# Silu as a product with a power, tile by tile: Exp on ScalarE, the rest on GpSimd

## The chip, the cores and the metric

One core of one Trainium2 chip runs the whole program in a single launch. The metric is the device time in microseconds. The engines are TensorE (PE in the rows), with its weight loads (PEld), VectorE (DVE), ScalarE (ACT), GpSimd (POOL) and SyncE (SP); each runs its own instructions in order and they meet at semaphores.

## The reference

Two transformer blocks are computed one after the other, on 512 tokens of width 1024 in float32. The change lies in the second block, in the branch beside its differential attention: a causal convolution of width 4 along the tokens, a Silu on it, and then projections to q and k of a recurrent cell:

```python
proj = u @ w_in[l]
qa, ka, va, xm, o_pre, ga, gb = jnp.split(proj, split_idx, axis=-1)
...
xc = jax.nn.silu(causal_conv(xm, conv_w, conv_b))
xch = xc.reshape(B, S, H, Dh)
q = jnp.einsum('bshd,hde->bhse', xch, w_mq)
k = jnp.einsum('bshd,hde->bhse', xch, w_mk)
```

Silu(x) is x / (1 + exp(-x)).

## The kernel before

Activations are held transposed: a tile has 128 features on the partitions and 512 tokens in its columns, so a width of 1024 is eight tiles. Each matrix product is made of three products in a rounded float format: the weights and the activations are each split into a high part (a rounded copy, made by ScalarE: `hi` for a chunk of weights, L564, and `split_hi` for an activation tile, L573) and a low part (the rest, made by VectorE: `lo`, L1925, and `split_lo`, L1931). A chunk of weights is 1024 x 128, and TensorE spends 24 products on it (L1138 to L1140).

The second attention has 32 units (four blocks of queries by eight heads). While TensorE works on a unit's scores, softmax and values, it also computes one of 32 side projections in each unit (the list `SIDE`: the two gates ga and gb, the output gate op, and xm), which fills its time. In unit i, TensorE runs projection i into bank 6 and, in the middle of it, the transposes of the weighted scores of unit i-1 (`turn`, L1692); then the scores of unit i+1 (L1684), in some units the transposes of a finished group (L1714), and the product with the values of unit i-1 (`av`, L1701). VectorE adds the mask and finds the maxima (L2469), splits weights (L1925), scales the second softmax (L2481) and writes the weighted difference of the two (L2484), which `turn` reads. ScalarE does the exponentials (L982), splits weights (L564), in every fourth unit squares and a Sqrt for the norm of a group (L955, L958), copies the transposed scores of unit i-1 (`mixed_out`, L972; `av` waits for it) and stores the side projection from the bank into a buffer (`store_side`, L949; the next projection waits for it). GpSimd sends each stored projection to memory (L2708).

The xm projections are those of units 5, 8, ... 26 (`XM_AT`). Their buffers are two (`xm_t`), taken in turn. VectorE convolves an xm tile into `E` in the three units behind it (`conv`, L2453 and L2455; semaphore `conv`). After all eight are convolved, in unit 31, ScalarE does the eight Silus in place (L993), between `mixed_out(30)` and the store of projection 31. Then, after `mixed_out(31)`, the eight tiles are split, and TensorE starts on the products for q and k, two tiles of x for each head.

The order around the Silus, on ScalarE:

```python
for i in range(UNITS + 1):
...
    if i:
        mixed_out(i - 1)
    if i == UNITS - 1:
        for kt in range(KT):
            act.wait_ge(s("conv"), kt + 1)
            A_(E[:, kt, :], E[:, kt, :], ACT.Silu).then_inc(s("xc_ready"), 1)
    if i < UNITS:
        act.wait_ge(chunk_done, C_SIDE + i + 1)
        store_side(i, bank[6][:, :])
```

Earlier in the program GpSimd has another task: it scales and adds up the modulation's weights, 128 x 1024 at a time (L2697, a multiply and an add with scalars; L2699, an add of two tiles), while VectorE works beside it on weights and hidden tiles.

Of the kernel before, what the change touches and what calls it, by code (L numbers as in the profile page):

```python
# [24 lines left out]
ALU = mybir.AluOpType  # L25
ACT = mybir.ActivationFunctionType
AX = mybir.AxisListType

P = 128
T = 512  # L30
META = 16
D = 1024
KT = D // P
# [38 lines left out]
XM_AT = [5 + 3 * k for k in range(8)]  # L72
# [6 lines left out]
def side_index(n):  # L79
    return sum(1 for x in SIDE[:n] if x[0] == SIDE[n][0])  # L80
# [65 lines left out]
def build(nc, t, out):  # L146
    ctx = ExitStack()
    with ctx:
        def sb(name, shape, dt=F32):
            return ctx.enter_context(nc.sbuf_tensor(name, shape, dt))  # L150

        def sem(name):
            return ctx.enter_context(nc.semaphore(name))

        bank = [ctx.enter_context(nc.psum_tensor(f"bank{b}", [P, T], F32)) for b in range(8)]
# [21 lines left out]
        def tiles(k, n):  # L177
            return tl(k, n).rearrange("p (a t) -> p a t", a=n)
# [25 lines left out]
        sinks = sb("sinks_b", [P, SH])  # L204
        own_head = sb("own_head", [P, 12])
        msel8 = sb("msel8", [P, P])
        eps = sb("eps", [P, 3])
        inv_d_gain = sb("inv_d_gain", [P, 16])
        gain23, wsq = inv_d_gain[:, 0:8], inv_d_gain[:, 8:16]
        comb = sb("comb", [P, 63])  # L210
# [13 lines left out]
        def s(name):  # L224
            if name not in S:
                S[name] = sem(name)
            return S[name]
# [55 lines left out]
        n = 0  # L283
# [118 lines left out]
        A, B, E = tiles(0, 8), tiles(8, 8), tiles(32, 8)  # L402
# [10 lines left out]
        pa_st = tl(42)  # L413
        xm_t = [tabs[:, k, 0:T] for k in range(2)]
        outst = [xm_t[side_index(n) % 2] if name == "xm" else tl(40 + n % 2) for n, (name, _) in enumerate(SIDE)]
        after = sb("after", [P, P])
        after_r = sb("after_r", [P, P], F32R)
# [130 lines left out]
        def _(act):  # L548
            link = Link(act, s("act_link"))
            A_ = nc.scalar.activation  # L550

            def hi(c, static=None):

                static = c if static is None else static
                if isinstance(c, int):
                    if c >= CHUNKS:
                        return
                    if c >= SPLITS:
                        act.wait_ge(chunk_done, c - SPLITS + 1)
                else:  # L560
                    i, per, base = c
                    act.wait_ge(chunk_done, i * per + (base - SPLITS + 1))
                wait_landed(act, c, static)
                A_(whi[:, static % SPLITS, :], stage[:, static % STAGES, :], ACT.Copy).then_inc(chunk_hi, 1)  # L564
# [3 lines left out]
            def split_hi(n, kt, src, shift=0.0):  # L568

                if n > 0 and kt == 0:  # L570
                    act.wait_ge(chunk_done, split_last[n - 1] + 1)
                if isinstance(shift, float):
                    ins = A_(xhi[:, kt, :], src, ACT.Copy)  # L573
                else:
                    ins = A_(xhi[:, kt, :], src, ACT.Identity, bias=shift)
                ins.then_inc(s("x_rounded"), 1)
# [362 lines left out]
            def store_side(n, b):  # L939

                if n >= 2:
                    act.wait_ge(s(f"spilled{n % 2}"), 16 * (n // 2))
                if n in XM_AT:
                    k = XM_AT.index(n)
                    if k < 2:
                        act.wait_ge(s("rot2_done"), 7)
                    else:
                        act.wait_ge(s("conv"), k - 1)
                A_(outst[n], b, ACT.Copy).then_inc(s("side_out"), 1)  # L949

            def group_squares(g):

                act.wait_ge(s("av_group"), g + 1)
                for q in range(4):
                    ins = A_(oa[g % 2][:, q * P:(q + 1) * P], bank[5][:, q * P:(q + 1) * P], ACT.Square, accum_out=ass_[:, q:q + 1])  # L955
                ins.then_inc(s("ass_ready"), 1)
                act.wait_ge(s("avar"), g + 1)
                A_(ass_[:, 4:8], ass_[:, 4:8], ACT.Sqrt).then_inc(s("astd"), 1)  # L958

            def group_out(g):  # L960
                b, hh = divmod(g, 2)
                act.wait_ge(s("oat_done"), g + 1)
                A_(A[:, 4 * hh:4 * hh + 4, b * P:(b + 1) * P], bank[7][:, :].rearrange("p (h q) -> p h q", h=4), ACT.Copy,
                   scale=sc[:, 63:64]).then_inc(s("ya_out"), 1)

            def mixed_out(i):

                b = i // AH
                act.wait_ge(s("at_t"), i + 1)
                if i >= 2:  # L970
                    act.wait_ge(s("av_done"), i - 1)
                A_(amT[i % 2][:, 0:b + 1, :], bank[4][:, 0:(b + 1) * P].rearrange("p (b q) -> p b q", q=P), ACT.Copy).then_inc(s("amt_out"), 1)  # L972

            UNITS = NB * AH
            for i in range(UNITS + 1):
                if i < UNITS:
                    b, h = divmod(i, AH)
                    N = (b + 1) * P
                    act.wait_ge(s("at_nm"), i + 1)
                    for c in range(2):  # L980
                        p = 2 * (i % 2) + c
                        ins = A_(ex[i % 2][c][:, 0:N], ex[i % 2][c][:, 0:N], ACT.Exp, bias=anm[:, p:p + 1], accum_out=asum[:, p:p + 1])  # L982
                    ins.then_inc(s("at_exp"), 1)
                    hi(C_SIDE + i + AHEAD)
                g, ph = divmod(i - 5, 4)
                if ph == 0 and 0 <= g < 7:
                    group_squares(g)
                if i:
                    mixed_out(i - 1)
                if i == UNITS - 1:  # L990
                    for kt in range(KT):
                        act.wait_ge(s("conv"), kt + 1)
                        A_(E[:, kt, :], E[:, kt, :], ACT.Silu).then_inc(s("xc_ready"), 1)  # L993
                if i < UNITS:
                    act.wait_ge(chunk_done, C_SIDE + i + 1)
                    store_side(i, bank[6][:, :])
                if ph == 0 and 0 <= g < 7:
                    group_out(g)


            for kt in range(KT):
                act.wait_ge(s("xc_ready"), kt + 1)
                split_hi(5, kt, E[:, kt, :])
            for m in range(3):
                if m == 2:
                    act.wait_ge(s("xm_in"), 16)
                    for kt in range(KT):
                        split_hi(6, kt, Dt[:, kt, :])
                for pair in range(2):
                    c = C_QKV + 2 * m + pair  # L1010
                    hi(c + AHEAD)
                    for q in range(4):
                        if q < 3:
                            act.wait_ge(s("qkv_done"), 3 * (c - C_QKV) + q + 1)
                        else:
                            act.wait_ge(chunk_done, c + 1)
                        A_((Ct, B, Dt)[m][:, 4 * pair + q, :], bank[q][:, :], ACT.Copy).then_inc(s("qkv_out"), 1)
                    if c == C_QKV:
                        group_squares(7)
                    if c == C_QKV + 1:  # L1020
                        group_out(7)
# [889 lines left out]
        def _(dve):  # L1911
            V = nc.vector
            link = Link(dve, s("dve_link"))
# [58 lines left out]
            V.memset(eps[:, 0:1], EPS1)  # L1972
            V.memset(eps[:, 1:2], EPS2)
            V.memset(eps[:, 2:3], EPS1 * EPS2)
            V.memset(comb[:, :], 0.0)
            V.memset(ss5, 1.0)
            link(V.memset(sc[:, 0:1], 0.0))
# [318 lines left out]
            for c in range(C_OUT1, C_FF1):  # L2296
                if c > C_OUT1:
                    lo(c + AHEAD)
                n = c - C_OUT1
# [137 lines left out]
            UNITS = NB * AH  # L2437
# [211 lines left out]
        def _(pool):  # L2649
            G = nc.gpsimd  # L2650
            link = Link(pool, s("pool_link"))
# [36 lines left out]
            for n in range(total):  # L2688
                m, kt = divmod(n, KT)
# [16 lines left out]
            for n, (name, _) in enumerate(SIDE):  # L2706
                pool.wait_ge(s("side_out"), n + 1)
                pool.dma_start(spill[name][side_index(n)], outst[n]).then_inc(s(f"spilled{n % 2}"), 16)  # L2708
            for q in range(2):
                pool.wait_ge(s(f"spilled{q}"), 8 * len(SIDE))  # L2710
            pool.wait_ge(s("av_done"), NB * AH)
# [54 lines left out]
```

## Time and profile before

| what | us |
|---|---|
| time, median of 3 runs | 2012.9 |
| lowest and highest run | 2012.11, 2016.67 |
| span of the profiled execution | 2012.8 |
| TensorE busy in it | 1962.5 (97%) |
| VectorE, ScalarE, GpSimd busy | 1144.1, 786.4, 366.4 |

The profile is of one execution, whose span is the time from its first to its last instruction. A row of a timeline gives a start and a duration in us, and in brackets how long the engine stood idle before it and for whom. Matmul rows overlap, so their spacing tells more than their duration. The second attention runs from about 1144 to 1391 us of the span.

### The profile page before, as it was taken

The numbers are of one execution on the slowest core, as the hardware profiler recorded it, in microseconds if no ns is written. First come the engines' busy times: TensorE is split into PE (matmuls) and PEld (weight loads), VectorE is DVE, ScalarE is ACT, GpSimd is POOL, SyncE is SP. The second block draws the span as 40 slices with busy tenths as digits, with TensorE's granted clock in tenths as the row PEclk, the third lists the DMA queues.
The fourth block names the chain that finished last, engine by engine and source line by source line (L and its number), as shares of the span: only waits on it lengthen the run. The fifth ranks groups of instructions, "written<-read, shape, count | busy, mean of one in ns | idle before, by whom it ended". The sixth has DMA issues, their size and how long they took to land.

```text
span 2012.8 us, 25489 instructions
## 1 busy us (share of the span) xinstructions
PE 1962.5 (97%) x9512; PEld 1572.4 (78%) x9512; DVE 1144.1 (57%) x1762; ACT 786.4 (39%) x1330; POOL 366.4 (18%) x298
## 2 busy tenths in 40 slices
PE   8999999999999999999999999999999999999998
PEld 6876678888887788888788877777677788888887
DVE  7566667667666655353564266665635755444444
ACT  7436442223225222222332345557756442222223
POOL 3000039999100694000000000000001000000000
PEclk9999999999999999999999999999999999999999
DMA  6320246666322664323245433323126423333331
GB/s 167 89 70 22 62 139 204 203 201 206 122 84 75 177 204 130 104 86 102 84 136 124 120 115 109 107 94 126 55 87 195 121 77 101 88 104 88 100 98 59
DMA packets 274989, 233.12 MB, mean 116 GB/s; under 512 B 16631, under 2 KB 248442, under 8 KB 274368
## 3 DMA queue, kind: packets, MB, share of 16 engines
q1 hardware_dynamic: 255792, 166.29, 28.3%
q0 software_dynamic: 17488, 60.36, 9.5%
q10 hardware_dynamic: 1632, 5.45, 1.1%
q8 instruction: 48, 0.79, 0.2%
q14 instruction: 29, 0.24, 0.0%
HBM read 214.95 MB, written 12.58 MB: 113 GB/s over the span
## 4 chain that ended last, share of the span: by engine, by line
PE 89%; DVE 5%; ACT 3%; issue 1%; DMA 1%; ACTq 0%; DVEq 0%; POOLq 0%
PE bank L1138 25%; PE bank L1140 24%; PE bank L1139 24%; PE bank L1144 2%; PE bank L1145 2%; DVE wlo L1925 1%; PE bank L1684 1%; PE bank L1701 1%; PE bank L1586 1%; PE bank L1842 1%; PE bank L1825 1%; PE bank L1355 1%; PE bank L1194 1%; PE bank L1507 1%; PE bank L1403 1%
## 5 line engine op out<-in xcount | busy, mean ns | idle before, releaser
L1138 PE MATMUL bank<-xhi,whi 128*128 128x512 f32 x1680 | 666.5, 397 | 5.5 <-PE bank L1701 2.4
L1140 PE MATMUL bank<-xhi,wlo 128*128 128x512 f32 x1680 | 656.4, 391 | 0.0
L1139 PE MATMUL bank<-xlo,whi 128*128 128x512 f32 x1680 | 655.3, 390 | 0.0
L1925 DVE TENSOR_TENSOR wlo<-stage,whi 128x1024 fp32r<-128x1024 f32 x309 | 406.4, 1326 | 207.7 <-ACT whi L564 207.3
L564 ACT ACTIVATE whi<-stage 128x1024 fp32r<-128x1024 f32 x309 | 321.2, 1051 | 403.3 <-PE bank L1140 365.0
L1138 PEld LDWEIGHTS bank<-xhi,whi 128*128 128x128 f32 x1680 | 316.3, 188 | 76.8 <-issue 9.9
L1140 PEld LDWEIGHTS bank<-xhi,wlo 128*128 128x128 f32 x1680 | 316.0, 188 | 68.1
L1139 PEld LDWEIGHTS bank<-xlo,whi 128*128 128x128 f32 x1680 | 316.4, 188 | 63.4
L2316 DVE SCALAR_TENSOR_TENSOR H<-bank,sc,H 128x512 f32<-128x512 f32 x304 | 217.9, 747 | 78.4 <-PE bank L1140 76.6
L1138 PE MATMUL bank<-hidhi,whi 128*128 128x512 f32 x532 | 209.5, 394 | 0.0
L1140 PE MATMUL bank<-hidhi,wlo 128*128 128x512 f32 x532 | 208.4, 392 | 0.0
L1139 PE MATMUL bank<-hidlo,whi 128*128 128x512 f32 x532 | 206.8, 389 | 0.0
L2338 DVE TENSOR_TENSOR arena<-bank,arena 128x512 f32<-128x512 f32 x44 | 30.5, 692 | 310.0 <-PE bank L1140 308.3
L2699 POOL TENSOR_TENSOR arena<-arena 128x1024 f32<-128x1024 f32 x63 | 167.9, 2666 | 5.3
L2684 POOL DMA_DIRECT2D arena<-in_w_ada x72 | 42.3, 588 | 430.6 <-DVE xlo L1931 259.0
L1140 PEld LDWEIGHTS bank<-hidhi,wlo 128*128 128x128 f32 x532 | 99.9, 188 | 23.2
L1139 PEld LDWEIGHTS bank<-hidlo,whi 128*128 128x128 f32 x532 | 99.9, 188 | 22.3
L1138 PEld LDWEIGHTS bank<-hidhi,whi 128*128 128x128 f32 x532 | 100.0, 188 | 20.3
L2697 POOL TENSOR_SCALAR arena<-arena,sc 128x1024 f32<-128x1024 f32 x72 | 105.1, 1460 | 5.6 <-DMA arena<-in_w_ada 2.5
L860 ACT ACTIVATE hidhi<-arena 128x512 fp32r<-128x512 f32 x44 | 27.9, 633 | 195.7 <-DVE arena L2338 195.7
L855 ACT ACTIVATE arena<-bank 128x512 f32<-128x512 f32 x44 | 26.4, 600 | 150.9 <-PE bank L1140 150.9
L2708 POOL DMA_DIRECT2D spill_ga<-arena x8 | 4.4, 552 | 415.3 <-ACT arena L949 415.3
(447 smaller groups left out, 2072.5 us busy)
## 6 DMA issues: line engine op xcount, KB each, us to landing
arena<-in_w_ada POOLq DMA_DIRECT2D x72, 512.0 KB, 4.0
stage<-in_w_in SPq DMA_DIRECT2D x71, 512.0 KB, 3.9
stage<-in_w_ff SPq DMA_DIRECT2D x64, 512.0 KB, 4.5
stage<-in_w_gate SPq DMA_DIRECT2D x44, 512.0 KB, 4.5
stage<-in_w_up SPq DMA_DIRECT2D x44, 512.0 KB, 3.9
stage<-in_w_down SPq DMA_DIRECT2D x44, 512.0 KB, 3.8
arena<-arena ACTq DMA_DIRECT2D x16, 256.0 KB, 5.4
stage<-in_w_proj_a SPq DMA_DIRECT2D x8, 512.0 KB, 4.1
```

The lines of the kernel that those rows point to most:

```text
L564: A_(whi[:, static % SPLITS, :], stage[:, static % STAGES, :], ACT.Copy).then_inc(chunk_hi, 1)
L1138: mm(out, sh, mh, start=start, stop=False, **kw)
L1139: mm(out, sh, ml, start=False, stop=False, **kw)
L1140: return mm(out, sl, mh, start=False, stop=stop, **kw)
L1144: mm(out, sh, mh, start=start, stop=False)
L1145: mm(out, sl, mh, start=False, stop=False)
L1925: V.tensor_tensor(wlo[:, static % SPLITS, :], stage[:, static % STAGES, :], whi[:, static % SPLITS, :].bitcast(F32), ALU.subtract).then_in ...
L2316: V.scalar_tensor_tensor(out=H[:, x, :], in0=bank[(4 + x) % 8][:, :], scalar=gate(x), in1=H[:, x, :], op0=ALU.mult, op1=ALU.add).then_inc( ...
L2338: V.tensor_tensor(hid_t[j], bank[2 * j + 1][:, :], act_t[j], ALU.mult).then_inc(hid_f32, 1)
L2684: pool.dma_start(st_ada[n % 3], t["w_ada_2"][0, kt * P:(kt + 1) * P, m * D:(m + 1) * D]).then_inc(ring[n % 3], 16)
L2697: link(G.tensor_scalar(dst, st_ada[n % 3], silu_c[:, kt:kt + 1], 0.0, ALU.mult, ALU.add))
L2699: G.tensor_tensor(acc, acc, t_ada, ALU.add).then_inc(s("ada_sum"), 1)
```

## The change

The Silu is taken apart. In units 9, 12, ... 30, one unit after a tile's convolution is finished, ScalarE writes exp(-x) into the xm buffer of that tile, which its spill and its convolution have read by then. GpSimd, behind the spill of the same unit, adds 1, takes the power -1 (against a column of -1 spread over the tile) and multiplies into `E`. The store of a later xm tile into the same buffer now waits for GpSimd's product. Behind the last unit ScalarE splits two tiles before `mixed_out(31)`, two after it, then stores projection 31, then splits the other four.

```diff
-        eps = sb("eps", [P, 3])
+        eps = sb("eps", [P, 4])
...
-                        act.wait_ge(s("conv"), k - 1)
+                        act.wait_ge(s("xc_ready"), k - 1)
...
+                if i == UNITS:
+                    for kt in range(2):
+                        act.wait_ge(s("xc_ready"), kt + 1)
+                        split_hi(5, kt, E[:, kt, :])
                 if i:
                     mixed_out(i - 1)
-                if i == UNITS - 1:
-                    for kt in range(KT):
-                        act.wait_ge(s("conv"), kt + 1)
-                        A_(E[:, kt, :], E[:, kt, :], ACT.Silu).then_inc(s("xc_ready"), 1)
-                if i < UNITS:
+                if i - 4 in XM_AT:
+                    k = XM_AT.index(i - 4)
+                    act.wait_ge(s("conv"), k + 1)
+                    A_(xm_t[k % 2], E[:, k, :], ACT.Exp, scale=-1.0).then_inc(s("xc_exp"), 1)
+                if i < UNITS - 1:
                     act.wait_ge(chunk_done, C_SIDE + i + 1)
                     store_side(i, bank[6][:, :])
...
-            for kt in range(KT):
+            for kt in range(2, KT):
                 act.wait_ge(s("xc_ready"), kt + 1)
                 split_hi(5, kt, E[:, kt, :])
+                if kt == 3:
+                    store_side(UNITS - 1, bank[6][:, :])
...
+            V.memset(eps[:, 3:4], -1.0)
...
                 pool.wait_ge(s("side_out"), n + 1)
                 pool.dma_start(spill[name][side_index(n)], outst[n]).then_inc(s(f"spilled{n % 2}"), 16)
+                if n - 4 in XM_AT:
+                    k = XM_AT.index(n - 4)
+                    e = xm_t[k % 2]
+                    pool.wait_ge(s("xc_exp"), k + 1)
+                    link(G.tensor_scalar(e, e, 1.0, 1.0, ALU.add, ALU.mult))
+                    link(G.tensor_tensor(e, e, eps[:, 3:4].to_broadcast([P, T]), ALU.pow))
+                    G.tensor_tensor(E[:, k, :], E[:, k, :], e, ALU.mult).then_inc(s("xc_ready"), 1)
```

## Rows read from the trace of the kernel before

**Rows 1.** The page: the span, and TensorE's busy time, share and instructions.

```profile
span 2012.8 us, 25489 instructions
...
PE 1962.5 (97%) x9512; PEld 1572.4 (78%) x9512; DVE 1144.1 (57%) x1762; ACT 786.4 (39%) x1330; POOL 366.4 (18%) x298
```

**Rows 2.** Stretches: length, each engine's busy time, TensorE's granted clock, DMA share, GB/s.

```profile
1150.00:1380.00 230.00, 225.37 (x1089) 169.50 (x1088) 141.51 (x373) 124.93 (x296) 16.88 (x31) 0.99 0.34 106
...
1387.00:1395.00 8.00, 4.57 (x19) 3.49 (x18) 4.11 (x7) 8.00 (x16) 1.46 (x2) 0.79 0.19 58
```

**Rows 3.** Timeline, TensorE, end of the attention: start, duration, line, tiles, idle before.

```profile
1385.31 0.39 PE L1139 MATMUL bank<-xlo,whi 128*128 128x512 f32 x1
1385.54 0.39 PE L1140 MATMUL bank<-xhi,wlo 128*128 128x512 f32 x1
...
1386.65 0.60 PE L1692 MATMUL bank<-ident,arena 128*128 128x128 f32 x4
1390.39 1.24 PE L1701 MATMUL bank<-arena 128*128 128x128 f32 x8 [3.13 <-ACT arena L972]
...
1392.49 0.63 PE L1139 MATMUL bank<-xlo,whi 128*128 128x512 f32 x1
1392.91 0.63 PE L1140 MATMUL bank<-xhi,wlo 128*128 128x512 f32 x1
```

**Rows 4.** Timeline, ScalarE, units 30 and 31 and the splits behind them.

```profile
1377.84 0.60 ACT L949 ACTIVATE arena<-bank 128x512 f32<-128x512 f32 x1 [1.86 <-PE bank L1140]
...
1383.81 1.28 ACT L993 ACT_TABLE_LOAD   x1
1385.11 4.27 ACT L993 ACTIVATE arena<-arena 128x512 f32<-128x512 f32 x8
...
1389.76 0.58 ACT L972 ACTIVATE arena<-bank 128x512 f32<-128x512 f32 x1
1390.24 4.26 ACT L573 ACTIVATE xhi<-arena 128x512 fp32r<-128x512 f32 x8
```

**Rows 5.** VectorE: the subtractions behind the splits (timeline), L1925 over the span (min/median/max ns).

```profile
1390.89 4.91 DVE L1931 TENSOR_TENSOR xlo<-arena,xhi 128x512 fp32r<-128x512 f32 x8 [5.14 <-ACT xhi L573]
...
L1925 DVE TENSOR_TENSOR wlo<-stage,whi x309: 1210/1224/3415, 12.5 to 1980.6; 128x1024 fp32r<-128x1024 f32 x155
```

**Rows 6.** Timeline, ScalarE: the stores of units 9, 11 and 27.

```profile
1214.37 0.60 ACT L949 ACTIVATE arena<-bank 128x512 f32<-128x512 f32 x1 [0.62 <-PE bank L1140]
...
1228.83 0.60 ACT L949 ACTIVATE tabs<-bank 128x512 f32<-128x512 f32 x1 [2.39 <-PE bank L1140]
...
1352.61 0.60 ACT L949 ACTIVATE arena<-bank 128x512 f32<-128x512 f32 x1 [2.17 <-PE bank L1140]
```

**Rows 7.** Timeline, GpSimd and VectorE behind the store of unit 30.

```profile
1378.73 0.54 POOL L2708 DMA_DIRECT2D spill_op<-arena  x1 [7.87 <-ACT arena L949]
...
1382.95 1.23 DVE L1925 TENSOR_TENSOR wlo<-stage,whi 128x1024 fp32r<-128x1024 f32 x1 [2.54 <-ACT whi L564]
...
1385.00 0.75 DVE L2484 SCALAR_TENSOR_TENSOR arena<-arena,small 128x512 f32<-128x512 f32 x1
```

**Rows 8.** GpSimd's two operations over the whole span: count, min/median/max ns, first, last.

```profile
L2697 POOL TENSOR_SCALAR arena<-arena,sc x72: 1127/1133/3182, 282.9 to 777.2; 128x1024 f32<-128x1024 f32 x72
...
L2699 POOL TENSOR_TENSOR arena<-arena x63: 2399/2412/3281, 287.0 to 778.5; 128x1024 f32<-128x1024 f32 x63
```

**Rows 9.** Timeline, GpSimd and VectorE side by side in the first block.

```profile
388.34 1.20 POOL L2697 TENSOR_SCALAR arena<-arena,sc 128x1024 f32<-128x1024 f32 x1
...
388.73 1.88 DVE L1925 TENSOR_TENSOR wlo<-stage,whi 128x1024 fp32r<-128x1024 f32 x1 [0.18 <-ACT whi L564]
...
389.62 3.24 POOL L2699 TENSOR_TENSOR arena<-arena 128x1024 f32<-128x1024 f32 x1
```

**Rows 10.** Timeline, TensorE: the transposes that need the weighted scores of units 10 and 28.

```profile
1225.64 0.38 PE L1692 MATMUL bank<-ident,arena 128*128 128x128 f32 x2
...
1365.97 0.60 PE L1692 MATMUL bank<-ident,arena 128*128 128x128 f32 x4
```

## The prediction

> **What bounds the kernel now.** I read the page first: a span of 2012.8 us and TensorE busy for 97% of it [rows 1]. So a change pays only where TensorE stands still, and costs only where it makes TensorE stand still. I then asked for the stretch that the diff touches, engine by engine. In the second attention, from 1150 to 1380 us, TensorE is busy 225.37 of 230 us and GpSimd 16.88 us, all of it the issuing of spills; from 1387 to 1395 us TensorE is busy only 4.57 of 8 us, at a granted clock of 0.79 [rows 2]. Next, the order of TensorE's work in that hole: the last transposes of the weighted scores (L1692) start at 1386.65 us and take 0.60, then it idles 3.13 us for ScalarE's copy of them (L972), does the last product with the values (L1701, 1.24 us), idles 0.30, and does six products at a spacing of 0.43 us, where it had 0.23 before the idle time [rows 3]. ScalarE's rows say why: after the copy for unit 30 it loads a table (1.28 us), does the eight Silus (4.27 us, 0.53 each), stores the last side projection, and only at 1389.76 copies for unit 31 [rows 4]. The Silus are the cause of the hole. The rest of the attention is bound by TensorE.
>
> **What the change takes away at the end.** The table load and the eight Silus leave that place, and the last store moves behind four splits. ScalarE then does two splits of x (0.53 us each) once projection 31 is done, near 1386.0, and has finished them when the transposes end at 1387.25. Its copy (0.58 us) ends at about 1387.95 and TensorE goes on at 1388.0 where it went on at 1390.39: 2.4 us won. VectorE subtracts behind each split at 0.61 us (4.91 us for eight, [rows 5]), so the first two tiles wait for nothing. If an idle time of 0.7 us leaves the clock up, six products at 0.23 for 0.43 give another 1.2. So the gain has a floor near 2.4 and a roof of 3.6 us.
>
> **What it adds on ScalarE.** Eight Exps of one 128x512 tile, at some 0.6 us like a store of that size [rows 4], in units 9, 12, ... 30. Ahead of the store of unit 27 ScalarE idles 2.17 us and ahead of that of unit 30 1.86 [rows 6, 4]; the Exp fits in. In units 9 and 21 a Sqrt stands before it, so the table load that now comes with the next softmax is drawn ahead: 1.28 + 0.6 = 1.9 us against 0.62 us of idle time in unit 9 [rows 6]. The store then ends some 1.3 us later; TensorE has the scores, a group's transposes and the values to do before it wants that bank, so I price it at 0 to 0.3 us, and take 0. One wait changes its meaning: the store of an xm tile waits for GpSimd's product of two tiles before, not for the convolution. The last spill is issued some 0.4 us earlier, and the read of xm that follows it is wanted only after four more chunks of products, so it keeps its room.
>
> **What it adds on GpSimd.** Three instructions for each tile, behind the spill of units 9, 12, ... 30. From the end of ScalarE's store of unit 30, 1378.44 us, it takes 0.29 us to the spill's issue and 0.54 for it [rows 4, 7]. 1+e is a two-step operation on 1024 columns at 1.13 us at the least, so about 0.57 on 512; the product at the end is half of 2.40, or 1.2 us [rows 8]. With two short gaps the power starts 1.5 us behind the store. No row shows a power. From below, it can't be quicker than that two-input operation: 1.2 us. From above, no row bounds it; I build it from L2697: two steps for 1024 columns in 1.13 us are 0.28 us for one step on 512. A power is a logarithm, a product and an exponential, each with a polynomial, a splitting of exponent and digits, and the special cases: I count some 42 steps, and would believe 28 to 64. That is an estimate of 12 us, from 8 to 18. I take 12, as the row nearest in kind is the same engine's arithmetic, not ScalarE's table.
>
> Whether that hurts is decided by VectorE. Where GpSimd runs beside it, one of the two stands still: L1925, two inputs in SBUF, normally 1.22 us, was at work from 388.73 for 1.88 us while L2697 ran until 389.54, which is the wait for its end and 1.07 us more; GpSimd's next operation was then stretched from 2.41 to 3.24 us [rows 8, 9]. The longest L1925 took 3.4 us [rows 5]. So I let VectorE's two-input operations wait for the whole power. The Trainium skill, SBUF — State Buffer, section "SBUF: two separate sides", calls the shared pair an exclusive lock held for the full instruction; the rows show that for operations of up to 2.4 us, and no row shows it for a long one.
>
> Who waits: L1925 of the next unit stands at the head of VectorE's queue, and behind it the scaling of the second softmax (L2481) and the weighting (L2484), and these make what TensorE transposes. In unit 31 L1925 starts at 1382.95 and the weighting ends at 1385.75 [rows 7]. After a power ends, VectorE needs about 1.1 us for L1925, lets GpSimd's product pass (1.2, partly beside small operations), and 1.2 for L2481 and L2484: 3.4 us. Free room is then the time from the store's end to TensorE's transposes, less 1.5 + 3.4. For the tile of unit 9: 1225.64 - 1214.97 - 4.9 = 5.8 us; for that of unit 27: 1365.97 - 1353.21 - 4.9 = 7.9; for that of unit 30: 1386.65 - 1378.44 - 4.9 = 3.3 [rows 3, 4, 6, 7, 10]. The same subtraction for units 12, 15, 18, 21 and 24 gives 6.3, 6.3, 6.3, 6.7 and 8.2.
>
> **The sum.** With 12 us for a power the first seven tiles cost 6.2 + 5.7 + 5.7 + 5.7 + 5.3 + 3.8 + 4.1 = 36.5 us, the last 8.7. Each stall of the first seven also drops the clock for some six products: 7 x 1.2 = 8.4 [rows 3]. At the end 2.4 is won; the clock falls there as before. 2012.8 + 36.5 + 8.7 + 8.4 - 2.4 = 2064. The span and the median of the runs (2012.9) are 0.1 us apart, so I leave it at 2064. With 8 us: 8.7 + 4.7 + 6 (five stalls with a fall of the clock) - 2.4 gives 2030; with 18 us: 78.5 + 14.7 + 8.4 - 2.4 gives 2112. GpSimd's spills of the two units behind come late by some 16 us, but the buffer that they free is wanted three units on, 24.6 us after the store of unit 27 [rows 4, 6].
>
> **Rivals.** (a) The power is cheap, up to 3.3 us. Then no tile waits, and the end gains 2.4 to 3.6: 2009.2 to 2010.4. It decides below 3.3 us. For it speaks that GpSimd stands idle and the tiles are three units apart; against it, that a two-input add alone takes 1.2 us. (b) A middle price, 3.3 to 7 us, if steps in a long program overlap so that one costs 0.14 us rather than 0.28 (42 steps: 5.9 us). Seven tiles are nearly hidden, and the last one's stall eats the gain: 5.9 - 3.3 - 2.4 = +0.2, so 2013. The Trainium skill's GPSIMD Engine Reference, section "Elementwise — side-by-side cycle accounting", has long bodies bound at roughly three operations a cycle of 1.2 GHz; by that an estimate for 42 steps is 6.0 us, and the time 2013. (c) The power holds VectorE up only while it fetches, not throughout. Then the return of the tile decides: 1.5 + 12 + 0.1 + 1.2 = 14.8 us behind the store of its unit; the buffer is wanted by the store two units on, which starts 13.9 us behind the end of unit 9's store [rows 6] and later than that for the rest, less some 1.2 us that TensorE has in hand; and the last tile is wanted by the last split near 1391.1, with some 2 us of cover from the first chunk's products. With 12 us that gives 2010 to 2013; with 18 us (20.8 us of return) about 5 us on six tiles and 7 at the end less 2.4, some 2045. Against it stand rows 9. (d) More than 64 steps: over 2112.
>
> **How the numbers follow.** The forecast, 8 to 18 us with the hold, has a chance of 0.45 (2030 to 2112). Cheap (a) 0.17, middle (b) 0.13, no hold (c) 0.13, dearer (d) 0.12. The predicted time is the forecast's, 2064. The range leaves out (d) and the edge of (a): 2008.5 to 2112. A measurement of this kernel can tell about 0.2%, 4 us, from no change. Faster by more needs all of the gain's roof and a little over, so half of (a) and little of (b) and (c): 0.13. Within 4 us: the rest of (a), most of (b), half of (c): 0.23. Slower: 0.45 + 0.12 and the rests of (b) and (c): 0.64.
>
> **What would show it.** The tensor-power rows on GpSimd give the price at once: about 12 us, eight of them. Beside each, one L1925 of VectorE should be as long as what is left of the power, and TensorE should idle for the weighting 4 to 6 us in the mid of the unit after next, at a lower clock behind it. At the end TensorE should wait about 0.7 us for the copy L972 once the transposes are done. The prediction is wrong if the power rows are under 7 us, or if L1925 keeps to 1.2 us beside a long one; then look at the xm stores in ScalarE's queue and at the last split.

## The result and the profile after

The changed kernel takes 2574.8 us (median of four runs, 2573.55 to 2580.6) where the kernel before takes 2014.52 beside it: a ratio of 1.2787, 95% interval 1.2769 to 1.2806. The forecast was 2064 us, the range ended at 2112. The sign was right, and the size was off by a factor of eleven (560 us against 51).

The page of the changed kernel: span, busy time of each engine, and the group of GpSimd that was not there before (count, then busy us and mean ns).

```profile
span 2571.7 us, 25512 instructions
...
PE 1977.2 (77%) x9512; PEld 1585.1 (62%) x9512; DVE 1146.2 (45%) x1763; ACT 784.7 (31%) x1329; POOL 1036.4 (40%) x322
...
L2721 POOL TENSOR_TENSOR tabs<-tabs,eps 128x512 f32<-128x512 f32 x8 | 655.6, 81949 | 0.7
```

Against [rows 1], VectorE and ScalarE have the same work as before; GpSimd has 670 us more, 655.6 of them in eight powers. One power of a 128x512 tile takes 81.95 us. It was the operation that no row of the kernel before showed and that the forecast put at 12 us.

GpSimd's timeline around the first tile (start, duration, line; in brackets the idle time before and its cause) shows what a power blocks:

```profile
1213.09 0.54 POOL L2715 DMA_DIRECT2D spill_ga<-arena  x1 [8.00 <-ACT arena L949]
1213.66 0.63 POOL L2720 TENSOR_SCALAR tabs<-tabs 128x512 f32<-128x512 f32 x1
1214.38 81.96 POOL L2721 TENSOR_TENSOR tabs<-tabs,eps 128x512 f32<-128x512 f32 x1
1296.42 1.26 POOL L2722 TENSOR_TENSOR arena<-arena,tabs 128x512 f32<-128x512 f32 x1
1297.62 0.63 POOL L2715 DMA_DIRECT2D spill_gb<-arena  x1
1298.70 0.55 POOL L2715 DMA_DIRECT2D spill_xm<-tabs  x1 [0.46 <-ACT tabs L949]
```

The spill of the next unit waits from about 1220 to 1297 us behind the power, and the store of the xm tile two units on waits for the product at 1296.42: it starts at 1297.79, and TensorE goes on at 1298.44. The waits of TensorE and of ScalarE over the attention (us in total, times, longest):

```profile
PE bank L1144 <- ACT tabs L949: 415.3, 6, 71.3
PE bank L1144 <- issue: 69.8, 1, 69.8
PE bank L1144 <- ACT arena L949: 61.9, 3, 61.2
...
ACT tabs L949 <- POOL arena L2722: 432.3, 6, 74.3
ACT xhi L573 <- POOL arena L2722: 71.8, 1, 71.8
ACT arena L949 <- DMA spill_op<-arena: 64.0, 1, 64.0
```

These eight waits are the loss. Six times ScalarE's store of an xm tile waits for GpSimd's product in the same buffer, and TensorE waits for the store: 415.3 us. Once (the tile of unit 27, whose buffer no later xm tile wants) the store of unit 30 waits for the spill of unit 28, which stood in GpSimd's queue behind the power: 61.2 us. And the last tile makes the last split late by 71.8 us. In ScalarE's queue the copies out of the banks (L1023) stand behind that split, and TensorE goes on at 1954.82, after the first of them: 69.8 us. The profile names no cause for this wait; ScalarE's rows give it:

```profile
1952.66 0.63 ACT L573 ACTIVATE xhi<-arena 128x512 fp32r<-128x512 f32 x1 [71.78 <-POOL arena L2722]
...
1954.15 2.04 ACT L1023 ACTIVATE arena<-bank 128x512 f32<-128x512 f32 x4
```

Together 415.3 + 61.2 + 69.8 = 546.3 us. TensorE's busy time has grown by 1977.2 - 1962.5 = 14.7 us. Part of that is the lower clock after each wait, here after the first (stretch, length, busy time of PE, PEld, DVE, ACT and POOL, then TensorE's granted clock, DMA share, GB/s):

```profile
1298.40:1301.60 3.20, 3.16 (x8) 2.49 (x9) 1.25 (x2) 1.91 (x5) 0.55 (x1) 0.50 0.43 164
1302.00:1306.00 4.00, 4.00 (x21) 2.99 (x20) 1.93 (x4) 0.91 (x3) 0.00 (x0) 1.00 0.46 133
```

After 71.28 us of standing still TensorE runs at 0.50 of full speed, 1.2 GHz, for some 3.2 us and then at 2.4 GHz. The hole of 3.13 us [rows 3] has shrunk to 0.69, so 2.4 us less. 2012.8 + 546.3 + 14.7 - 2.4 = 2571.4, against a span of 2571.7. That the sum closes so well is partly luck: between executions without any such wait the busy time differs by up to 9 us (1957.0 us in the run silu_tile below, 1965.8 in tanh).

VectorE, which the forecast had made the sufferer, wasn't held. L1931 is the split of weights (L1925 before); first all of it between 1205 and 1960 us (min/median/max ns), then one that ran inside the first power:

```profile
L1931 DVE TENSOR_TENSOR wlo<-stage,whi x25: 1224/1226/1309, 1207.4 to 1959.7; 128x1024 fp32r<-128x1024 f32 x25
...
1215.40 1.23 DVE L1931 TENSOR_TENSOR wlo<-stage,whi 128x1024 fp32r<-128x1024 f32 x1 [2.11 <-ACT whi L564]
```

At 1215.40, 1 us into a power that lasts until 1296.34, it takes its 1.23 us. The contrast with [rows 9] is what the experiments had to explain.

### The profile page after: what moved, and what is told of

Same layout as the page of the kernel before. It is cut to its first block, busy times and chain, and to the rows that moved or that the text cites. A ratio compares the mean times of both kernels' runs of the same rounds, so it can differ in the third digit from the quotient of the medians.

```text
span 2571.7 us, 25512 instructions
## 1 busy us (share of the span) xinstructions
PE 1977.2 (77%) x9512; PEld 1585.1 (62%) x9512; DVE 1146.2 (45%) x1763; ACT 784.7 (31%) x1329; POOL 1036.4 (40%) x322
## 4 chain that ended last, share of the span: by engine, by line
PE 65%; POOL 23%; DVE 4%; issue 4%; ACT 2%; DMA 1%; ACTq 0%; DVEq 0%; POOLq 0%
POOL tabs L2721 22%; PE bank L1144 19%; PE bank L1146 18%; PE bank L1145 18%; PE bank L1150 1%; PE bank L1151 1%; DVE wlo L1931 1%; PE bank L1592 1%; PE bank L1848 1%; PE bank L1361 1%; PE bank L1831 1%; PE bank L1200 0%; PE bank L1513 0%; PE bank L1409 0%; DMA arena<-spill_pa 0%
## 5 line engine op out<-in xcount | busy, mean ns | idle before, releaser
L1144 PE MATMUL bank<-xhi,whi 128*128 128x512 f32 x1680 | 674.4, 401 | 551.6 <-ACT tabs L949 415.3
L1931 DVE TENSOR_TENSOR wlo<-stage,whi 128x1024 fp32r<-128x1024 f32 x309 | 407.1, 1328 | 681.2 <-ACT whi L564 680.9
L2721 POOL TENSOR_TENSOR tabs<-tabs,eps 128x512 f32<-128x512 f32 x8 | 655.6, 81949 | 0.7
```

The source lines that it names most:

```text
L1144: mm(out, sh, mh, start=start, stop=False, **kw)
L1931: V.tensor_tensor(wlo[:, static % SPLITS, :], stage[:, static % STAGES, :], whi[:, static % SPLITS, :].bitcast(F32), ALU.subtract).then_in ...
L2721: link(G.tensor_tensor(e, e, eps[:, 3:4].to_broadcast([P, T]), ALU.pow))
```

## The experiments

The first four runs below are one execution each, beside one of the kernel before (2016.2 us). All executions of that kernel lie between 2010.0 and 2019.7 us, so where a time differs from it by less than some 10 us, only the rows decide.

Two theories stood after the result. A: a power has a high price for each column, leaves VectorE alone, and costs what its late return makes others wait. B: the forecast's own step, that VectorE is held by it. Beside them: that the price is fixed for an instruction or belongs to this exponent, these numbers or this form of operand, and that the rest of the change costs something too.

**What a power costs (cols).** The power becomes a power to 1 on a part of each tile, and a Tanh makes the Silu right without it.

```diff
-  A_(xm_t[k % 2], E[:, k, :], ACT.Exp, scale=-1.0)
+  A_(xm_t[k % 2], E[:, k, :], ACT.Tanh, scale=0.5)
...
-  V.memset(eps[:, 3:4], -1.0)
+  V.memset(eps[:, 3:4], 1.0)
...
-  link(G.tensor_scalar(e, e, 1.0, 1.0, ALU.add, ALU.mult))
-  link(G.tensor_tensor(e, e, eps[:, 3:4].to_broadcast([P, T]), ALU.pow))
+  link(G.tensor_scalar(e, e, 1.0, 0.5, ALU.add, ALU.mult))
+  w = (512, 256, 128, 64, 32, 16, 4, 1)[k]
+  link(G.tensor_tensor(e[:, 0:w], e[:, 0:w], eps[:, 3:4].to_broadcast([P, w]), ALU.pow))
```

> Base: Tanh in place of Exp and 0.5(1+e) in place of the power, so that the tiles come out right; then a power (to 1, which changes nothing) on the first 512, 256, 128, 64, 32, 16, 4 and 1 columns of tile 0, 1, ... 7. Theory A (the price is per column, 81.95/512 = 0.16 us each, and what it costs is the tile's late return): powers of 82, 41, 20.5, 10.2, 5.1, 2.6, 0.6 and 0.2 us; TensorE idles 71 us for the return of tile 0, 29 for tile 1, 8 to 9 for tile 2, nothing from 64 columns down; time 2013 + 109 + 3 clock losses of 1.8 - 3.6, some 2123. Rival C (most of the price is fixed for an instruction): all eight near 80 us, time near 2570. Rival B (the power stops VectorE's two-input operations): beside the 512-column power one of L1925's rows is tens of us long.

The timeline of GpSimd, the eight powers alone, and TensorE's wait for the stores:

```profile
1216.08 81.97 POOL L2722 TENSOR_TENSOR tabs<-tabs,eps 128x512 f32<-128x512 f32 x1
...
1310.53 41.15 POOL L2722 TENSOR_TENSOR tabs<-tabs,eps 128x256 f32<-128x256 f32 x1
...
1364.64 20.74 POOL L2722 TENSOR_TENSOR tabs<-tabs,eps 128x128 f32<-128x128 f32 x1
...
1398.61 10.55 POOL L2722 TENSOR_TENSOR tabs<-tabs,eps 128x64 f32<-128x64 f32 x1
...
1423.46 5.45 POOL L2722 TENSOR_TENSOR tabs<-tabs,eps 128x32 f32<-128x32 f32 x1
...
1445.57 2.93 POOL L2722 TENSOR_TENSOR tabs<-tabs,eps 128x16 f32<-128x16 f32 x1
...
1471.63 1.03 POOL L2722 TENSOR_TENSOR tabs<-tabs,eps 128x4 f32<-128x4 f32 x1
...
1496.86 0.57 POOL L2722 TENSOR_TENSOR tabs<-tabs,eps 128x1 f32<-128x1 f32 x1
...
PE bank L1144 <- ACT tabs L949: 108.3, 3, 71.3
```

A straight line: 81.97 - 41.15 = 40.82 us for 256 columns, 0.159 us each, and about 0.4 us for the instruction. Of the three waits, 71.3 us belong to 512 columns; TensorE's idle times in the same trace give 29.2 us for 256 and 7.8 for 128, where theory A said 29 and 8 to 9, and from 64 columns down no store is waited for. The time is 2128.32 us against 2123 expected, 112 over the kernel before beside it against 110 expected. So a wait follows from the length of the power and the room of the tile, as rival (c) of the forecast has it; the price put into that rule was wrong.

**Does the price depend on what is raised to what (forms)?** With the Tanh, eight operations of 64 columns on a scratch tile:

```diff
+  by = [eps[:, c:c + 1].to_broadcast([P, 64]) for c in range(3, 7)]
+  b_, r_ = base[:, :], res[:, :]
...
+  if k == 0:
+      link(G.tensor_tensor(r_, b_, by[0], ALU.pow))
+  elif k == 1:
+      link(G.tensor_tensor(r_, b_, expo[:, :], ALU.pow))
+  elif k == 2:
+      link(G.tensor_tensor(r_, b_, by[1], ALU.pow))
...
```

> Same base with Tanh; beside the right result GpSimd does one 64-column operation on a scratch tile for each of the eight tiles, and nobody reads it: power by -1 from a spread column, -1 from a full tile, 2, 0.5, 1, -1 of a tile of ones, -1 on 16 partitions only, and an add. Theory A, a fixed program per column: the six on 128 partitions all 10.2 us whatever exponent, number or operand form; the one on 16 partitions the same (each core does its own partitions); the add under 0.4 us. Rival C2 (the price is that of the special exponent, of the numbers or of the spread operand): the rows differ by a factor of two or more. Time: each return is 1.5 + 0.3 + 10.2 + 0.8 + 1.3 = 14.1 us against 13.9 to 16.5 of room, so nothing is waited for: 2009 to 2013.

GpSimd's groups (lines in no order of time; L2734 is -1, L2736 -1 from a full tile, L2738 2, L2740 0.5, L2742 1, L2744 a tile of ones, L2746 16 partitions, L2748 the add):

```profile
L2736 POOL TENSOR_TENSOR res<-base,expo 128x64 f32<-128x64 f32 x1 | 10.6, 10587 | 0.1
L2744 POOL TENSOR_TENSOR res<-base,eps 128x64 f32<-128x64 f32 x1 | 10.6, 10582 | 0.1
L2734 POOL TENSOR_TENSOR res<-base,eps 128x64 f32<-128x64 f32 x1 | 10.6, 10567 | 0.1
L2740 POOL TENSOR_TENSOR res<-base,eps 128x64 f32<-128x64 f32 x1 | 10.6, 10558 | 0.1
L2746 POOL TENSOR_TENSOR res<-base,eps 16x64 f32<-16x64 f32 x1 | 10.6, 10555 | 0.1
L2738 POOL TENSOR_TENSOR res<-base,eps 128x64 f32<-128x64 f32 x1 | 10.5, 10549 | 0.1
L2742 POOL TENSOR_TENSOR res<-base,eps 128x64 f32<-128x64 f32 x1 | 10.5, 10547 | 0.1
...
L2748 POOL TENSOR_TENSOR res<-base,expo 128x64 f32<-128x64 f32 x1 | 0.3, 317 | 0.1
```

All seven powers take 10.55 to 10.59 us: none of the four exponents is a short cut, a tile of ones is no cheaper, and 16 partitions cost what 128 do. The add takes 0.32. The time is 2013.93 us beside 2016.2 of the kernel before. ScalarE's stores wait for a tile four times (10.4 us in all, 3.2 at most), but TensorE has work for so long: it waits for such a store once, 0.26 us. So seven powers of 10.6 us cost almost nothing, and are near the edge.

**Does a power hold VectorE (aside)?** The kernel before, and on GpSimd eleven powers that nobody waits for:

```diff
   pool.dma_start(spill[name][side_index(n)], outst[n]).then_inc(s(f"spilled{n % 2}"), 16)
+  if 9 <= n < 30 and n % 2:
+      link(G.tensor_tensor(aside[:, :], aside[:, :], eps[:, 3:4].to_broadcast([P, 80]), ALU.pow))
```

> The kernel before, with its Silus where they were; GpSimd does, behind the spills of units 9, 11, ... 29, a power on 80 columns of a scratch tile that nobody reads: eleven of 12.8 us, the price that the forecast took. Theory A (VectorE isn't held): time of the kernel before, within 2 us, and L1925 at 1.22 us throughout. Rival B (VectorE's two-input operations wait for the power): each power ends 13.7 us behind its store, the weighted scores come at 16 us against 10.7 to 13.1: 3 to 5 us eleven times and a fall of the clock each, some 2065, and eleven L1925 of 8 to 11 us.

The power (min/median/max ns) and the split of weights (here L1926) between 1200 and 1450 us:

```profile
L2713 POOL TENSOR_TENSOR aside<-aside,eps x11: 13125/13126/13235, 1216.2 to 1371.3; 128x80 f32<-128x80 f32 x11
...
L1926 DVE TENSOR_TENSOR wlo<-stage,whi x30: 1221/1226/1227, 1204.6 to 1428.0; 128x1024 fp32r<-128x1024 f32 x30
```

Eleven powers of 13.13 us, and the longest of the 30 splits takes 1.227. The time is 2015.16 us, beside 2016.2. Theory B falls: with powers of about the price that the forecast took (12 us), VectorE's splits lose nothing.

**And an ordinary stream (aside_mul)?** The same places, five products of 1024 columns instead:

```diff
+  if 9 <= n < 30 and n % 2:
+      aside = hidhi[:, :, :].rearrange("p a t -> p (a t)")
+      for _ in range(5):
+          link(G.tensor_tensor(aside, aside.bitcast(F32), ones[:, 0:1].to_broadcast([P, 1024]), ALU.mult))
```

> The same with five two-input products of 1024 columns (2.4 us each, 12 us together) in place of each power, on a hidden tile that is not in use then, multiplied by ones. If what held VectorE in the first block is a two-input stream of GpSimd: L1925 up to 3.4 us and others likewise in the units with products; a unit's chain of VectorE is 3 to 6 us longer against 4 to 5 us of room, so the time is 0 to 20 us over that of the kernel before. If GpSimd's work beside the attention held VectorE in general, the powers of the run beside this one do the same.

GpSimd's five products and VectorE's operations beside them (timeline), then what TensorE waited for:

```profile
1229.67 10.18 POOL L2712 TENSOR_TENSOR hidhi<-hidhi,ones 128x1024 fp32r<-128x1024 f32 x5
...
1229.42 2.19 DVE L2479 TENSOR_TENSOR small<-small,sc 128x1 f32<-128x1 f32 x1
1231.64 2.06 DVE L2481 TENSOR_SCALAR arena<-arena,small 128x256 f32<-128x256 f32 x1
1233.74 2.07 DVE L2484 SCALAR_TENSOR_TENSOR arena<-arena,small 128x256 f32<-128x256 f32 x1
...
1238.02 0.41 DVE L2469 CUSTOM_DVE_ANT_0 arena<-bank,arena 128x256 f32<-128x256 f32 x1
...
PE bank L1692 <- DVE arena L2484: 23.0, 10, 4.0
PE bank L1701 <- ACT arena L972: 14.9, 11, 3.5
PE bank L1714 <- DVE gg L2444: 10.8, 5, 3.4
```

An operation of VectorE on a single column, 0.16 us in the runs with a power, takes 2.19 beside a product of 2.03 us (the mean of all 55); each of the next two waits for one product too. Not every operation is held: L2469, which reads a bank of TensorE and a tile, keeps its 0.41 us while the last product still runs, and none of its 46 rows between 1200 and 1450 us is longer than in the kernel before (0.69 us). TensorE waits ten times for the weighted scores, as the forecast described it. The time is 2074.23 us, 58 over the kernel before, more than the 0 to 20 that I expected; the rows show small operations held for a whole product each. So the hold is real, it comes with the products and not with the powers, and for like durations (10 to 13 us in every second unit) the products cost 58 us and the powers nothing that can be told.

**What the rest of the change is worth (tanh, tanh_old_end).** Without a power, with Tanh as above; the second also goes back to the old order behind the last unit:

```diff
-                if i == UNITS:
-                    for kt in range(2):
-                        act.wait_ge(s("xc_ready"), kt + 1)
-                        split_hi(5, kt, E[:, kt, :])
...
-                if i < UNITS - 1:
+                if i < UNITS:
...
-                if kt == 3:
-                    store_side(UNITS - 1, bank[6][:, :])
```

> The change without a power: Silu(x) = x * 0.5 * (1 + tanh(x/2)), Tanh on ScalarE in the Exp's place, 0.5(1+e) and the product on GpSimd. Theory A (the power is the whole loss, and the rest is worth what the end of the attention gives): 2.4 to 3.6 us under the kernel before, ratio 0.9982 to 0.9988. Rival D (the eight functions in ScalarE's units, GpSimd's products or the new order cost too): the same as before or slower.

> The same with the old order behind the last unit: store 31, the copy for unit 31, then the eight splits. If the gain is the removal of the Silus from there, this keeps all but 0.5 us of it, as the copy starts when the transposes end and the first split comes at 1388.4 by the clock of the kernel before, with its subtraction at 1389.0, about when TensorE has the values done. If the two early splits are what wins, it loses 1 us or more of it.

The ratios are 0.9993 (0.9982 to 1.0004) and 0.9987 (0.9975 to 0.9999). So what is left of the change is a gain of some 0.1%, which in the changed kernel's own order can't be told from none, and the two orders can't be told apart by time. The trace with the old order has the same idle time of 0.69 us ahead of the last product with the values as the changed kernel. The two early splits win nothing that can be seen.

**Silu itself, moved (silu_tile, silu_old_end).** No Exp, nothing on GpSimd; the Silu of each tile in the Exp's place, with the new order and with the old one:

```diff
-  A_(xm_t[k % 2], E[:, k, :], ACT.Exp, scale=-1.0).then_inc(s("xc_exp"), 1)
+  A_(E[:, k, :], E[:, k, :], ACT.Silu).then_inc(s("xc_ready"), 1)
...
```

> Silu itself in the Exp's place, tile by tile on ScalarE, nothing on GpSimd. Each brings two table loads of 1.28 us, one ahead of it and one ahead of the next softmax. ScalarE's idle time ahead of the store is 1.9 to 2.4 us in most of these units, the softmax has 4 to 5 us of room: if these rooms are right, 2 to 3.6 us are won as with Tanh. If the softmax is late (its room was misread), 1.3 us are lost eight times: 7 us slower than with Tanh.

> Silu tile by tile on ScalarE in the middle of the attention, as in the run silu_tile, and the old order behind the last unit: nothing is left of the change but where the Silus stand. If the hole behind the Silus was the whole gain to be had (3.6 us), this has it: TensorE idles 0.7 us for the last copy and goes on at the full clock, ratio 0.998 to 0.9995. If the early splits were needed, TensorE idles 1 us or more before the products for q.

0.9987 (0.9976 to 0.9999) and 0.9982 (0.9972 to 0.9992): the second is 2011.26 us beside 2015.3. It beats both kernels, and it differs from the kernel before only in where the eight Silus stand (and in an unused column of constants). The wait for the last copy, and, from the run silu_tile, ScalarE's rows in a unit with a Silu:

```profile
PE bank L1701 <- ACT arena L972: 0.7, 1, 0.7
...
1347.23 1.28 ACT L997 ACT_TABLE_LOAD   x1
1348.53 0.64 ACT L997 ACTIVATE arena<-arena 128x512 f32<-128x512 f32 x1
1349.36 0.60 ACT L949 ACTIVATE arena<-bank 128x512 f32<-128x512 f32 x1 [0.20 <-PE bank L1146]
1349.98 1.28 ACT L982 ACT_TABLE_LOAD   x1
```

The table load and the Silu fill the time in which ScalarE would have idled before its store, and the load back falls into the room of the softmax.

**The reciprocal on VectorE (recip).** In place of GpSimd's three operations:

```diff
+  dve.wait_ge(s("xc_exp"), k + 1)
+  link(V.tensor_scalar(e, e, 1.0, None, ALU.add))
+  link(V.reciprocal(e, e))
+  V.tensor_tensor(E[:, k, :], E[:, k, :], e, ALU.mult).then_inc(s("xc_ready"), 1)
```

> Exp on ScalarE as in the change; 1+e, reciprocal and product on VectorE in the unit behind, nothing on GpSimd. No row shows a reciprocal of 512 columns; the 4-column ones take 0.18 us. At one column a cycle as the other operations, the three take 0.35 + 0.6 + 0.7 us and fit in VectorE's room of 4 to 5 us: 2.4 to 3.6 us won. If the reciprocal takes 4 us or more, up to 1 to 3 us are lost in each of eight units and it is slower than before.

The reciprocal's row (min/median/max ns):

```profile
L2504 DVE RECIPROCAL tabs<-tabs x8: 3352/3352/3354, 1219.7 to 1409.4; 128x512 f32<-128x512 f32 x8
```

3.35 us is under the 4 us from which I expected a loss, and still the ratio is 1.0113 (1.0092 to 1.0134): 23 us over the kernel before, an expectation that missed. The loss isn't even. TensorE waits 18.6 us in six places for the scaling of a finished group (L2451), where the kernel before has 2.0; in the two longest, 5.8 and 6.2 us, a reciprocal stands ahead of that scaling in VectorE's queue. So the room of 4 to 5 us that I took for every unit wasn't there in these two.

## Why the prediction was right or wrong

- **The hole behind the Silus: right in the rows, its worth borne out by another run.** TensorE's rows at the end of the changed kernel's attention:

```profile
1876.57 0.60 PE L1698 MATMUL bank<-ident,arena 128*128 128x128 f32 x4
1877.86 1.16 PE L1707 MATMUL bank<-arena 128*128 128x128 f32 x8 [0.69 <-ACT arena L972]
1879.32 0.47 PE L1144 MATMUL bank<-xhi,whi 128*128 128x512 f32 x1 [0.30 <-DVE xlo L1937]
1879.62 0.40 PE L1145 MATMUL bank<-xlo,whi 128*128 128x512 f32 x1
```

  0.69 us of idle time instead of 3.13 [rows 3], and a granted clock of 1.00, 2.4 GHz, from 1876 to 1885 us, where [rows 2] has 0.79 over the hole. That is the roof of 3.6 us, and silu_old_end measures 4 us, with an interval from 1.6 to 5.6 (0.9982 of 2015). The changed kernel's own end, in the run tanh, gives 0.7 in a thousand, which can't be told from nothing.
- **What it adds on ScalarE: right.** The Exp makes the store of unit 9 late, and TensorE waits 0.24 us for it, within the 0 to 0.3 us allowed; no later unit shows such a wait, in the run tanh neither, where no power hides one.
- **GpSimd around the power: right.** The power of the second tile starts 1.57 us behind its store (1.5), 1+e takes 0.63 us (0.57), the product 1.26 (1.2).
- **The price of the power: the step that failed.** I counted 42 steps at 0.28 us for 512 columns. 81.95 us are some 290 such steps. With the price goes the range: its upper end, 18 us, was only the upper end of the count. The count was a guess about a program whose length no row shows, and the bounds of 28 to 64 gave a guess the look of a range; an operation without a row should have been left open above, with the point where it begins to cost (some 14 us of return) as the only firm number. The Trainium skill's GPSIMD Engine Reference, section "Elementwise — side-by-side cycle accounting", has about three operations a cycle for long bodies; my 42 steps at that rate gave an estimate of 6.0 us, and the measured 82 us decide against the count, the rate or both.
- **VectorE held for the whole power: the second step that failed.** All the stalls of the sum were of this kind (36.5 us for the first seven tiles, 8.7 for the last), and none of them happened. (The terms of the 3.4 us behind a power add up to 3.5, which changes little.) The rows of before were read rightly and carried over to an operation of another kind. aside_mul has the hold, aside and the changed kernel have not: 1.23 us for a split beside powers of 13 and 82 us. The Trainium skill, SBUF — State Buffer, section "SBUF: two separate sides", has the lock held for the full instruction; for products the runs agree (0.16 us became 2.19), for powers of 13 and 82 us they don't. Why a power leaves the port free is not settled: that it fetches its operands early and then computes would fit, and wasn't tried.
- **Rival (c), the late return, took its place.** With the measured price the first tile's return is 1.5 + 82 + 0.1 + 1.3 = 84.9 us against 13.9 of room: 71.0 us, and 71.3 were measured. The 1.2 us that TensorE was to have in hand, which the rule takes off as well (69.8), did not show there. I had given it 0.13 and priced it at 12 and 18 us only. The forecast's signs of being wrong did name this place: the xm stores in ScalarE's queue and the last split.
- **The spills: wrong at 82 us.** I let them be late because their buffer is wanted 24.6 us on; one of the eight waits (61.2 us) is just that. Beside the powers of 13 us in aside no store waits for a spill.
- **The fall of the clock behind a stall: right in kind.** After the first wait the rows show some 3.2 us at 1.2 GHz, so 1.6 us lost, against 1.2 estimated. The 14.7 us of busy time over eight waits would be 1.8 each, but a few us of them may be the difference between two executions.

No run has a power of 12 us on the path. In cols TensorE's waits are 10.7, 11.9 and 12.9 us shorter than the powers of the first three tiles, so 12 us would have cost an estimated 1.4 us there and won 2.4 to 3.6 at the end: about the kernel before, or a little faster.

## What to carry to other kernels

Before work is moved to an idle engine, its price there has to come from a row; where none shows it, the honest answer is the price at which it begins to cost, and a range that is open above. An idle engine that hands its result back in a small ring of buffers stops the whole pipeline as soon as its return takes longer than the ring goes round, here two units. When a function's own place is the trouble, try moving it first: the eight Silus one unit behind their convolutions, with table loads and all, won what the rewriting was after, some 4 us of 2015.

## What the runs showed of the hardware

- A power on GpSimd takes 0.4 us and 0.159 us for each column (0.57 us for one, 81.97 for 512). At 64 columns it is the same for the exponents -1, 0.5, 1 and 2, for a spread column and a full tile of exponents, for a tile of ones, and on 16 partitions as on 128 (10.55 to 10.59 us).
- GpSimd's product of 1024 columns can hold an operation of VectorE on tiles for its own length, down to one on a single column (0.16 us became 2.19), while one that reads a bank as well keeps its 0.41 us. Powers of 13 us hold none of 30 splits of weights (1.227 us at the most).
- A reciprocal of 128x512 on VectorE takes 3.35 us, where a product of two such tiles takes 0.69 in the same run.
- A table load on ScalarE in the middle of its work costs its 1.28 us and no more, in the rows shown: it starts 0.01 us after the end of the operation ahead of it, and the Silu starts 1.30 us after the load does.
